# Attention of a hybrid trunk: scores computed a second time, turned, in place of transposing the exponentials

## The reference, cut to what matters

```python
def fox_prompt(q, k, v, logf):
    cum = cumsum(logf)                       # per head, over positions
    s = einsum(q, k) * 64 ** -0.5
    s = s + cum[query] - cum[key]
    s = where(query >= key, s, NEG_INF)
    return softmax(s) @ v

def fox_sample(q, k, v, logf, ck, cv, clogf):
    # the same with keys, values and logf of the cache ahead of the 64 new ones
```

## Time and profile before

| | |
|---|---|
| Median of 3 runs | 4307.74 us (4306.70 to 4316.57) |
| The profiled execution | 4307.08 us, its span 4305.3 us |
| TensorE busy | 3881.8 us, 90% of the span |
| VectorE, ScalarE, GpSimd busy | 1410.7, 871.5 and 222.4 us |
| Attention, prompt: first score to last copy | 382.6 to 739.9 us |
| Attention, sample | 740.2 to 842.9 us |
| Mean granted TensorE clock | 0.909 of 2.4 GHz |

### The profile page before, as it was taken

One profiled execution on the slowest core, in us unless ns is written; L12 is line 12 of the kernel. 1 busy time (PEld: TensorE's weight loads), 2 busy tenths in 40 slices (PEclk: granted clock), 3 DMA queues, 4 the chain that ended last, 5 costly groups with the idle time before them and its releaser, 6 DMA issues.

```text
span 4305.3 us, 64869 instructions
## 1 busy us (share of the span) xinstructions
PE 3881.8 (90%) x27636; PEld 3357.1 (78%) x27636; DVE 1410.7 (33%) x1926; ACT 871.5 (20%) x1206; POOL 222.4 (5%) x375
## 2 busy tenths in 40 slices
PE   7999998699999999896899785888878999999988
PEld 5996665588999999783466455777766999999967
DVE  2133222234221222533200563555465222222352
ACT  2001222222000000214401341333333010010020
POOL 0001000000000000000000111111110000000000
PEclk9997555799999999997799897999988999999999
DMA  2211001311112113111322562111131111211311
GB/s 88 81 44 32 10 10 52 114 60 55 44 47 83 44 43 120 36 42 40 120 71 76 201 235 79 52 52 52 49 118 67 44 44 61 69 44 40 127 35 66
DMA packets 75663, 295.54 MB, mean 69 GB/s; under 512 B 9473, under 2 KB 11793, under 8 KB 71233
## 3 DMA queue, kind: packets, MB, share of 16 engines
q0 software_dynamic: 37136, 169.82, 11.0%
q1 hardware_dynamic: 38336, 122.87, 9.0%
HBM read 216.03 MB, written 76.62 MB: 68 GB/s over the span
## 4 chain that ended last, share of the span: by engine, by line
PE 84%; DVE 8%; issue 3%; ACT 2%; DMA 1%; POOL 0%; SPq 0%; DVEq 0%; ACTq 0%; POOLq 0%
PE ps L408 51%; PE ps L382 11%; PE ps L513 3%; PE ps L536 2%; DVE A L1368 2%; PE ps L768 2%; PE ps L777 2%; DVE B L1368 1%; PE ps L682 1%; PE ps L523 1%; PE ps L422 1%; PE ps L480 1%; DVE A_r L1425 1%; PE ps L728 1%; PE ps L440 1%
## 5 line engine op out<-in xcount | busy, mean ns | idle before, releaser
L408 PE MATMUL ps<-A_r,TM_r 128*128 128x364 f32 x2736 | 605.8, 330 | 0.0
L408 PE MATMUL ps<-H_r,W_r 128*128 128x364 f32 (+1 forms) x2616 | 576.7, 329 | 0.0
L408 PE MATMUL ps<-H_r,TM_r 128*128 128x364 f32 x2352 | 521.2, 330 | 18.1 <-DVE A_r L1425 18.1
L382 PE MATMUL ps<-B,W 128*128 128x364 f32 (+1 forms) x1488 | 467.9, 475 | 24.9 <-DVE B L1368 24.9
L408 PEld LDWEIGHTS ps<-A_r,TM_r 128*128 128x128 f32 x2736 | 476.4, 189 | 0.0
L408 PEld LDWEIGHTS ps<-H_r,W_r 128*128 128x128 f32 (+1 forms) x2616 | 454.0, 187 | 1.8
L382 PEld LDWEIGHTS ps<-B,W 128*128 128x128 f32 (+1 forms) x1488 | 281.4, 190 | 206.8 <-issue 27.0
L408 PEld LDWEIGHTS ps<-H_r,TM_r 128*128 128x128 f32 x2352 | 408.4, 188 | 22.4 <-issue 14.4
L408 PE MATMUL ps<-B_r,DW_r 128*128 128x364 f32 x2112 | 408.9, 329 | 0.0
L408 PE MATMUL ps<-B_r,W_r 128*128 128x364 f32 x1824 | 404.6, 330 | 0.0
L408 PEld LDWEIGHTS ps<-B_r,DW_r 128*128 128x128 f32 x2112 | 358.8, 188 | 0.0
(11 more groups left out here) (281 smaller groups left out, 4475.3 us busy)
## 6 DMA issues: line engine op xcount, KB each, us to landing
W<-in_wgu SPq DMA_DIRECT2D x88, 512.0 KB, 3.5
W<-in_wdown SPq DMA_DIRECT2D x32, 384.0 KB, 3.1
W<-in_wrkv SPq DMA_DIRECT2D x24, 512.0 KB, 3.5
W<-in_wdown SPq DMA_DIRECT2D x32, 320.0 KB, 2.9
d_h<-H POOLq DMA_DIRECT2D x16, 546.0 KB, 3.0
d_y<-TM POOLq DMA_DIRECT2D x16, 546.0 KB, 3.4
A<-d_y POOLq DMA_DIRECT2D x16, 546.0 KB, 8.1
H<-d_h POOLq DMA_DIRECT2D x2, 4368.0 KB, 22.7
```

What stands on the lines that cost most here:

```text
L382: ins = nc.tensor.matmul(ps[0:cols, NCH * s + c, 0:CH], W[0:rows, slot, j * cols:(j + 1) * cols], xs[n][0:rows, c * CH:(c + 1) * CH], star ...
L408: ins = nc.tensor.matmul(ps[0:cols, NCH * s + c, 0:CH], w[:, j * cols:(j + 1) * cols], x[k1][:, c * CH:(c + 1) * CH], start=(k1 == 0 and n ...
```

## The change

The whole attention is replaced; nothing outside it is changed but the waits at its ends. Scores are computed twice:

1. As before, queries in partitions, in 12 pieces of up to 512 keys a pair (ROWS). VectorE only takes their maximum with the bias (`reduced`); what it writes (DUMP) is not used. The maxima TOP have one column for each query block.
2. **Turned**: keys in partitions, queries along the free dimension, in 12 groups a pair (COLS: the half f of the queries, 512 wide, and the key block kb; c0 is the first query column that isn't wholly masked). VectorE adds the key's cum as a number per partition (CKT) and subtracts the maximum, spread over partitions (`shifted`), and ScalarE takes the exponential in place.

`spread` makes the maxima of a half a row in all partitions: a matmul with the TOP column, repeated 128 times, as stationary operand and the identity moving, and a ScalarE copy to MB. `turn_sums` turns the cum rows once for all heads. `values` has the 64 columns of values as the stationary operand (bank 6) and then 64 columns of ones (bank 7), so bank 7 gets the softmax's sums, and the output comes out with features in partitions as B wants it: no transposes are left. `total` turns the sums into 1/sum by Ln and Exp, and `scaled` writes the output. The two heads of a pair are alternated, matmul by matmul, and their operands are read from B without staging.

The sample's turned scores are 17 blocks of 128 keys a pair, in 5 groups; its bias for the maxima comes from a matmul with SEL (8 partitions, picks the head's cum) into the same bank.

One step j of pair p is, on each engine in this order: the group two ahead (turned; shifted; exponential), piece j of the next pair's scores and maxima, and the values of group j. The first pair's scores and maxima run alone ahead of all. `full_clock` has 16 matmuls instead of 28.

```diff
 # TensorE
-            def scores(u, b):
...
-            def turn_exp(u):
...
-            def values(u, b):
...
-            def turn():
...
+            def scores(p, j):
+                qb, n0, n = ROWS[j]
+                if pieces(p, j):
+                    pe.wait_ge(S["s_read"], pieces(p, j))
+                if halves(p, int(j >= FIRST_HALF[0])):
+                    pe.wait_ge(S["mb_read"], halves(p, int(j >= FIRST_HALF[0])))
+                q, diag = P0 + P * qb, n0 + n == P * (qb + 1)
+                for h, r in enumerate(HEAD):
+                    ins = nc.tensor.matmul(ps[:, h, 0:n], B[r, p, q:q + P], B[r, NA + p, P0 + n0:P0 + n0 + n],
+                                           start=True, stop=not diag, skip_group_check=True)
+                if diag:
+                    for h in range(2):
+                        ins = nc.tensor.matmul(ps[:, h, n - P:n], identb[:, :], causb[:, 0:P],
+                                               start=False, stop=True, skip_group_check=True)
+                ins.then_inc(S["s_done"], 1)
+            def scores_cache(i, j):
...
+                pe.wait_ge(S["s_read"], pieces(p, j) - (1 if j else 0))
...
+                nc.tensor.matmul(ps[:, j % 2, 0:n], QN[:, i, :], keys, start=True, stop=False, skip_group_check=True)
+                ins = nc.tensor.matmul(ps[:, j % 2, 0:n], SEL[:, i, :], cumk[:, 512 * j:512 * j + n],
+                                       start=False, stop=j < NGRP - 1, skip_group_check=True)
...
+            def spread(p, f):
+                if p < NA:
+                    pe.wait_ge(S["s_read"], pieces(p, len(ROWS) if f else FIRST_HALF[0]))
...
+                    for h in range(2):
+                        for a in range(4):
+                            col = TOP[p % 2][h][:, 4 * f + a:4 * f + a + 1]
+                            ins = nc.tensor.matmul(ps[:, h, P * a:P * a + P], col.to_broadcast([P, P]), k("ident"),
+                                                   start=True, stop=True)
...
+            def turned(p, j):
+                g = groups(p, j)
+                if g >= 2:
+                    pe.wait_ge(S["x_ready"], 2 * (g - 1))
+                st = 2 + 2 * (g % 2)
+                if p < NA:
+                    f, kb, c0 = COLS[j]
+                    key, q, diag = P0 + P * kb, P0 + 512 * f, kb >= 4 * f
+                    for h, r in enumerate(HEAD):
+                        ins = nc.tensor.matmul(ps[:, st + h, c0:512], B[r, NA + p, key:key + P], B[r, p, q + c0:q + 512],
+                                               start=True, stop=not diag, skip_group_check=True)
+                    if diag:
+                        for h in range(2):
+                            ins = nc.tensor.matmul(ps[:, st + h, c0:c0 + P], causb[:, 0:P], identb[:, :],
+                                                   start=False, stop=True, skip_group_check=True)
+                else:
...
+                            ins = nc.tensor.matmul(ps[:, st, P * a:P * a + P], CK[i][:, P * (4 * j + a):P * (4 * j + a) + P],
+                                                   QN[:, i, :], start=True, stop=True)
...
+            def values(p, j):
+                g = groups(p, j)
+                pe.wait_ge(S["e_ready"], 2 * (g + 1))
+                if p < NA:
+                    f, kb, c0 = COLS[j]
+                    if kb == 0 and halves(p, f):
+                        pe.wait_ge(S["o_read"], halves(p, f))
+                    for bank in (6, 7):
+                        for h, r in enumerate(HEAD):
+                            w = Vt[:, kb, P * p + C * h:P * p + C * h + C] if bank == 6 else k("ones")[:, 0:C]
+                            ins = nc.tensor.matmul(ps[r, bank, c0:512], w, EXP[g % 3][:, h, c0:512], start=(kb == 0),
+                                                   stop=(kb == 4 * f + 3), skip_group_check=True)
...
-            full_clock(28)
+            full_clock(16)
+            turn_sums()
+            for j in range(len(ROWS)):
+                scores(0, j)
+                if j == FIRST_HALF[0] - 1:
+                    spread(0, 0)
+            spread(0, 1)
+            turned(0, 0)
+            turned(0, 1)
+            for p in range(2 * NA):
+                for j in range(GROUPS[p]):
+                    if ahead(p, j):
+                        turned(*ahead(p, j))
+                    if p + 1 < NA:
+                        if j == FIRST_HALF[0]:
+                            spread(p + 1, 0)
+                        scores(p + 1, j)
+                        if j == len(ROWS) - 1:
+                            spread(p + 1, 1)
+                    elif p + 1 < 2 * NA:
+                        for piece in range(2 * j, min(NGRP, 2 * j + 2)):
+                            scores_cache(p + 1 - NA, piece)
+                        if j == NGRP // 2:
+                            spread(p + 1, 0)
+                    values(p, j)
 # VectorE
+            def reduced(p, j):
...
+                for h in range(2):
+                    top = TOP[p % 2][h][:, qb:qb + 1]
+                    ins = nc.vector.tensor_tensor_reduce(out=DUMP[h][:, 0:n], in0=ps[:, h, 0:n], in1=BIAS[2 * p + h][:, n0:n0 + n],
+                                                         scale=1.0, scalar=top if n0 else -3e38, op0=ALU.add, op1=ALU.max,
+                                                         accum_out=top)
+                ins.then_inc(S["s_read"], 1)
+            def shifted(p, j):
...
+                    for h in range(2):
+                        stt(EXP[g % 3][:, h, c0:512], ps[:, st + h, c0:512], CKT[:, kb, 2 * p + h:2 * p + h + 1],
+                            MB[f][:, h, c0:512], ALU.add, ALU.subtract).then_inc(S["x_ready"], 1)
...
+            def scaled(p, f):
...
+                nc.vector.tensor_tensor(B[:, 12 + p % NA, at:at + n], ps[:, 6, 0:n], RTOT[:, 0:n],
+                                        ALU.mult).then_inc(S["o_read"], 1)
+            for j in range(len(ROWS)):
+                reduced(0, j)
...
+                    if ahead(p, j):
+                        shifted(*ahead(p, j))
+                    if p + 1 < NA:
+                        reduced(p + 1, j)
 # GpSimd
-            def stage_prompt(i):
...
-            def stage_sample(i):
...
+            for i in range(NA):
+                if i:
+                    pool.wait_ge(S["bias_in0"], 32 * i)
                 for h in range(2):
+                    pool.dma_start(BIAS[2 * i + h], d_c[i:i + 1, h, :].to_broadcast([P, SEQ])).then_inc(S["bias_in0"], 16)
...
+            for i in range(2):
+                pool.wait_ge(S["s_read"], pieces(2 * i + 2))
+                sample_cache(i)
```

More of the change, by code:

```diff
@@ L244, in build_trunk, with pieces, groups, halves @@
         eLC = sb("eLC", [P, NPAIR, NCHUNK + 1])
+        def pieces(p, j=0):
+            return sum(PIECES[:p]) + j
+        def groups(p, j=0):
+            return sum(GROUPS[:p]) + j
+        def halves(p, f=0):
+            return sum(HALVES[:p]) + f
+        def ahead(p, j):
+            j += 2
+            if j >= GROUPS[p]:
+                p, j = p + 1, j - GROUPS[p]
+            return (p, j) if p < 2 * NA else None
         def k(name):
@@ L541, in turn, with turn_sums @@
[L541 to L544 removed]
+            def turn_sums():
+                pe.wait_ge(S["cum_ready"], 1)
+                for blk in range(8 + NBLK):
+                    n = P if blk < 8 + NBLK - 1 else C
+                    cum = Tf[0:HF, NALL + P * blk:NALL + P * blk + n] if blk < 8 else Tf[0:HF, P * (blk - 8):P * (blk - 8) + n]
+                    ins = nc.tensor.matmul(ps[0:n, 2, HF * blk:HF * blk + HF], cum, k("ident")[0:HF, 0:HF], start=True, stop=True)
+                ins.then_inc(S["ckt_done"], 1)
@@ L1032, in _ @@
-            with t.loop(2, p_ready=32, e_ready=32, pt_done=32, pt_read=32, o_done=32, ot_done=16, ot_read=16) as i:
-                for b in range(2):
-                    pair = i * 2 + b
-                    exp_of(0)
-                    exp_of(1)
-                    for u in range(16):
-                        turned(u)
-                        if u + 2 < 16:
-                            exp_of(u + 2)
-                        if u % 2 == 0 and u:
-                            output_block(pair, u // 2 - 1)
-                        t.up("o_done")
-                    output_block(pair, 7)
@@ new lines, in total @@
+            def total(p, f, last):
+                n = 512 if p < NA else C
+                act.wait_ge(S["v_done"], groups(p, last) + 1)
+                if halves(p, f):
+                    act.wait_ge(S["o_read"], halves(p, f))
+                nc.scalar.activation(RTOT[:, 0:n], ps[:, 7, 0:n], ACT.Ln).then_inc(S["r_log"], 1)
+                act.wait_ge(S["r_log"], halves(p, f) + 1)
+                nc.scalar.activation(RTOT[:, 0:n], RTOT[:, 0:n], ACT.Exp, scale=-1.0).then_inc(S["r_ready"], 1)
@@ L1583, in _ @@
+            dve.wait_ge(S["o_read"], halves(2 * NA))
             t.up("h_in", 16)
```

425 lines of the change are left out of this document (179 added, 246 removed).

## The result

| | before | after |
|---|---|---|
| Median | 4307.74 us | 4124.79 us (3 runs, 4123.89 to 4134.79) |
| Ratio | | 0.9577, 95% interval 0.9547 to 0.9606 |
| Span of the profiled execution | 4305.3 us | 4122.3 us |
| Mean granted TensorE clock | 0.909 | 0.951 |
| Output projection behind the attention starts at | 845.50 us | 693.01 us |

The change takes 183 us away, where I forecast 120 and left room down to 4150. The direction was as forecast, and so was what happens in the attention. The size was not: 152.5 us come from the attention, and 30.5 from work behind it, whose code is the same in both.

The account below looks back on a forecast made before the run. TensorE bounds the attention, 90 us a prompt pair at half clock. The new stage's terms sum to 330.5 us, ending at 713; the gain of 129.8, less 10 for clock falls, gives 4188 us, range 4150 to 4265.

Parts of the forecast that it names:

- Allowance for falls of the clock: Attention stage: the recurrence's clock of 0.97 and the pipeline's waits cost a few per cent of 275 us, 10 us.
- gain 129.8: Attention stage: 460.3 us now, ending at 713 instead of 842.9, before 10 us is taken off for the clock.
- The start: First pair's scores and maxima alone: 50 us at half clock, TensorE busy less than half; 34 at full clock.
- The pair: Prompt pair at full clock: 46.0 us of TensorE work and two stalls of 2.5, so 51 us for 90 now.
- my sign of being wrong: Main loop: clock 0.5, a 512-column step over 4.5 us at full clock, or TensorE waiting mostly for VectorE.
- The overlap: Attention matmuls: two heads of 512 columns stream side by side in 0.87 us, 31.2 us a pair instead of 62.5.
- Rival "don't overlap": Attention matmuls: heads don't overlap at 512 columns, 31 us more a pair, kernel 4320 or down to 4295; chance 0.06.
- The sample: Sample pairs in the attention: 22 us each including waits of 2.5, three times 66, the last 11.5 without cache scores.
- The cache scores: Sample pair: 4 pieces of 4 records of 0.434 us and 0.35 around each, put at 8.9 us.
- The clock: New attention steps: filling both halves of the array with 512 columns a load gives full clock, with short falls.
- removing them raises the clock whatever fills the time: Attention transposes, 12.5% of the stage's chain: by the skill's rule, taking them out lifts the half clock regardless of replacement.
- The steps as a chain: Attention steps: hand-overs between three engines make them 4.7 to 5 us, 60 a pair, kernel 4239; chance 0.14.

Follow-up runs that it names:

- experiment 1: Empty TensorE instructions ahead of layer 1's recurrence: kernel before with 37 or 128, 4278.32, 4315.50 us; changed kernel with 219, 128 or 256, 4162.83, 4168.54, 4135.36 us.
- experiments 2 and 4: Changed kernel with the heads' matmuls less alternated, 4197.56 us, or another step order, 4132.98 us; and, in experiment 4, both heads' scores read from head 0, 4201.57 us.
- experiment 4: Kernel before, transposes as ordinary matmuls, 4239.08 us, or left out, 4213.73; changed kernel, both heads' scores from head 0, 4201.57, or prompt values left out, 4124.23.

## Why the prediction was wrong, step by step

| Term | forecast | measured | less by |
|---|---|---|---|
| First scores to first turned group | 50 | 428.35 - 382.61 = 45.7 | 4.3 |
| Fill and pairs 0 to 2 | 158 | 578.68 - 428.35 = 150.3 | 7.7 |
| Pair 3, to its last values | 43 | 621.20 - 578.68 = 42.5 | 0.5 |
| Sample, end | 79.5 | 689.67 - 621.20 = 68.5 | 11.0 |
| From there to the projection | 2.6 | 693.01 - 689.67 = 3.3 | -0.7 |
| Allowance for falls of the clock | 10 | in the rows above | 10 |
| All behind the stage | 0 | 4122.3 - 693.01 against 4305.3 - 845.50 | 30.5 |

The sum, 63.3, is the miss (4188 for 4124.8). The start of the sum is the first scores before; 578.68 is the end of the last spread. No single term explains the miss: with only the 30.5 us behind the stage the time would have been 4157.5, and with only the 32.8 within it 4155, both inside the range.

- **The step that failed** is "gain 129.8", taken as the whole kernel's because the code outside the stage is the same: the term for the work behind the stage was put at nothing, and measured 30.5. The recurrence got 28.3 us shorter. Gaps that the profile before already showed as "issue" went from 40.2 to 14.5 us, waits for other engines took some of that back, and experiment 1 moved the length both ways by position alone. I read the recurrence only for its rates, not for its idle time.
- **The start** came out 4.3 us shorter than forecast and for nearly the reasons given, with the clock at 0.54. But TensorE was busy 28.5 of 44 us, not less than half.
- **The pair** was right at 46.0 + 5: 49.3 and 50.9, with TensorE busy 44.7 of 49. VectorE's 29.4 was 27.0, ScalarE's bound of 19 was 16.2. The spread's wait was 1.5, that of the first values 1.8 and that for the copy to MB 1.2, together 4.5, where I had 2.5 twice. By the letter of my sign of being wrong, TensorE does wait mostly for VectorE (some 12 of 15.6 us from 428 to 622), but the waits are only 8% of that time.
- **The overlap** was right: 0.91 us for four records of 512 columns. Rival "don't overlap" is out by these starts and by experiments 2 and 4.
- **The sample** was mis-sized: a pair takes 19.1 us (the spreads at 635.09 and 654.19) for 22, since the waits that I put at 2.5 are mostly covered, and the values' records start 31 ns apart (28 of them from 626.23 to 627.10) for the 38 from the earlier trace rows. The wait that remains there is 0.39. The cache scores were also added up wrong: 4 pieces of 4 x 0.434 and 0.35 make 8.3, not 8.9.
- **The clock** came out as forecast, for a reason that was half right. Streaming both halves of the array did carry it (0.54 at the start, 0.98 behind), but either kind of new work would have. The row of one head's scores at half clock was no guide: in experiment 4 such scores ran at 0.89 to 1.00. The allowance of 10 us was too much: at 0.98 over 263 us the loss is about 5 us, an estimate, and it stands in the rows above. The rule of the Trainium skill, "TensorE: Matmul & The Clock Gate", Part 4, that transposes don't count as work, agrees with experiment 4, where ordinary matmuls in their place raised the clock and leaving them out did nothing. My reading of it, that "removing them raises the clock whatever fills the time", was wrong.
- **The steps as a chain** (0.14) was out; the start was such a chain, and was priced as one.

## What to carry to other kernels

An edit that changes an engine's instruction count moves all code behind it in the instruction stream. Where a long run of short instructions shows idle time put down to "issue", compare its length before and after, apart from the edited stage, and try some empty instructions ahead of it before crediting or blaming the edit: here 37 of them were worth as much as a sixth of the whole change. For the clock, ask what work is left, and not only what is taken out. Where two engines hand one buffer back and forth, try a second buffer before another order of the hand-overs: here 18.5 us against 5. And keep full-array matmuls out from between two that should run side by side.

## What the runs showed of the hardware

- The same stretch of matmuls took 454.1 us, and 492.3, 476.8 and 455.3 with 128, 219 and 256 empty instructions ahead of it; over all kernels 451.3 to 493.2.
- 310 of 315 unexplained gaps of TensorE there ended 1.2 to 2.3 us after a 16.4 KB packet of the instruction queue had landed.
- Two heads' values products of 512 columns took 1.87 us in either order of the list; a full-array matmul between two heads' scores of 512 columns made 2.43 us of 1.28.
- Turning by ordinary float32 matmuls, twice the records, made the old stage 37 us faster than turning by transposes: its clock was 0.72 for 0.55.
- At half clock, leaving out 72 transposes a pair gave 17.2 us a pair (90 to 72.8) and nothing of the clock, 0.50 in both.
- Work in one half of the array only (scores of one head) ran at 0.89 to 1.00 when values products of 512 columns stood between, and at 0.50 when these had 64 columns.
